# Idle TensorE products in the opening's waits, and vector steps put in another order, in a fused one-layer kernel

## What is computed

```python
sh1, sc1, g1, sh2, sc2, g2 = adaln(cond, w_ada, b_ada)     # SiLU(cond) @ w_ada + b_ada
h = modulate(x, norm1_g, sh1, sc1)                         # rmsnorm(x) * (1 + scale) + shift
qkv, z, bl, al, na, gt = split_in(h, w_in)
o_dn, s = deltanet_branch(qkv, z, bl, al, ...)             # chunked gated DeltaNet, 8 heads
o_na = na_latent(...)                                      # neighbourhood attention, 8 heads
x = x + g1 * ((sig(gA) * (o_dn @ w_pa) + sig(gB) * (o_na @ w_pb)) @ w_out)
x = x + g2 * swiglu(modulate(x, norm2_g, sh2, sc2), w1, w3, w2)   # 2816 hidden features
```

## Time and profile before

| what | value |
|---|---|
| timed, median of 3 runs | 1314.75 us (1313.21 to 1315.12) |
| profiled execution, its own time | 1316.9 us |
| span of its profile | 1315.1 us |
| mean granted TensorE clock | 0.993 |
| PE busy | 98% |
| PEld busy | 93% |
| DVE busy | 74% |
| ACT busy | 53% |
| POOL busy | 13% |

### The profile page before, as it was taken

One profiled execution on the slowest core, in us unless ns is written; L12 is line 12 of the kernel. 1 busy time (PEld: TensorE's weight loads), 2 busy tenths in 40 slices (PEclk: granted clock), 3 DMA queues, 4 the chain that ended last, 5 costly groups with the idle time before them and its releaser, 6 DMA issues.

```text
span 1315.1 us, 25980 instructions
## 1 busy us (share of the span) xinstructions
PE 1294.9 (98%) x9834; PEld 1220.3 (93%) x9834; DVE 971.0 (74%) x2230; ACT 700.5 (53%) x1578; POOL 171.1 (13%) x161
## 2 busy tenths in 40 slices
PE   6999999999999999999999999999999999999998
PEld 4898999999999999999988889999999999999998
DVE  6677867777685867767447666767999698987995
ACT  4564736465464646555366654437564355534643
POOL 1002020202002020200202220000103300041022
PEclk7999999999999999999999999999999999999999
DMA  9743534334143333315425225522323323233223
GB/s 313 238 129 96 163 103 118 109 101 117 48 136 101 114 103 96 98 53 149 145 72 191 67 77 167 159 61 57 87 75 97 91 70 97 65 97 97 76 61 105
DMA packets 207860, 144.59 MB, mean 110 GB/s; under 512 B 9471, under 2 KB 197159, under 8 KB 207607
## 3 DMA queue, kind: packets, MB, share of 16 engines
q1 hardware_dynamic: 207447, 142.79, 37.0%
q10 hardware_dynamic: 288, 0.13, 0.0%
HBM read 126.73 MB, written 17.99 MB: 110 GB/s over the span
## 4 chain that ended last, share of the span: by engine, by line
PE 93%; DVE 3%; DMA 1%; issue 1%; ACT 1%; SPq 1%; DVEq 0%; ACTq 0%
PE ps L1304 33%; PE ps L1927 26%; PE ps L1671 7%; PE ps L1586 3%; PE ps L1907 2%; PE ps L1278 2%; PE ps L1526 2%; PE ps L1593 2%; PE ps L1409 1%; PE ps L1605 1%; PE ps L1780 1%; PE ps L1766 1%; PE ps L1812 1%; PE ps L1886 1%; PE ps L1604 1%; PE ps L1664 1%
## 5 line engine op out<-in xcount | busy, mean ns | idle before, releaser
L1304 PE MATMUL ps<-hT_r,WAH_r 128*128 128x320 f32 x624 | 155.1, 330 | 0.0
L1304 PE MATMUL ps<-xT_r,WAH_r 128*128 128x320 f32 x624 | 142.5, 310 | 0.0
L1927 PE MATMUL ps<-d_part_r,W_r 128*128 128x320 f32 x660 | 136.8, 310 | 1.1 <-DVE xT L3365 0.7
L1304 PE MATMUL ps<-hT_r,W_r 128*128 128x320 f32 x592 | 134.7, 311 | 0.0
L1927 PEld LDWEIGHTS ps<-d_part_r,W_r 128*128 128x128 f32 x660 | 107.5, 188 | 2.2 <-DVE xT L3365 1.5
L1304 PEld LDWEIGHTS ps<-hT_r,WAH_r 128*128 128x128 f32 x624 | 100.9, 190 | 9.2 <-issue 8.2
L1927 PE MATMUL ps<-t_big_r,W_r 128*128 128x320 f32 x380 | 107.5, 310 | 0.9 <-DVE c L3341 0.7
L1304 PEld LDWEIGHTS ps<-xT_r,WAH_r 128*128 128x128 f32 x624 | 105.1, 189 | 0.0
L1927 PE MATMUL ps<-b_part,W_r 128*128 128x320 f32 x456 | 101.2, 309 | 0.0
L1304 PEld LDWEIGHTS ps<-hT_r,W_r 128*128 128x128 f32 x592 | 99.5, 190 | 0.1
L1927 PE MATMUL ps<-t_small_r,W_r 128*128 128x320 f32 x304 | 93.9, 309 | 0.0
(11 more groups left out here) (483 smaller groups left out, 3447.6 us busy)
## 6 DMA issues: line engine op xcount, KB each, us to landing
oT<-in_ffn_w SPq DMA_DIRECT2D x44, 512.0 KB, 5.1
W<-in_w_in SPq DMA_DIRECT2D x36, 512.0 KB, 4.7
WAH<-in_w_ada SPq DMA_DIRECT2D x16, 1024.0 KB, 7.3
naT<-in_w_in SPq DMA_DIRECT2D x24, 512.0 KB, 4.2
ext_dram<-naT SPq DMA_DIRECT2D x28, 320.0 KB, 4.1
oT<-in_ffn_w SPq DMA_DIRECT2D x32, 256.0 KB, 4.0
tA<-ext_dram SPq DMA_DIRECT2D x16, 320.0 KB, 4.1
GCB<-gc_dram SPq DMA_DIRECT2D x7, 640.0 KB, 4.6
```

Source lines behind the costliest of these rows:

```text
L1304: m = e.matmul(ps[:, bank + b, 0:n], w[:, k, :], x[:, k, a:a + n], start=k == 0 and i == 0, stop=k == KD - 1 and i == 2, skip_group_check= ...
L1927: m = e.matmul(ps[:, bank, 0:HT], w[i][:, k, :], x[i][:, k, :], start=start and k == 0 and j == 0, stop=k == half - 1 and j == 2, skip_gro ...
```

## The change

Seven places of the program are touched; GpSimd's and SyncE's instructions stay as they are.

1. **Opening, TensorE.** A new function `stay_busy(count)` issues `count` products of the 128 by 128 identity with itself into an unused PSUM bank, each in float32. There are 7 between the halves of `ada_group(0)`, 2 ahead of `ada_select(0)`, 9 behind it, and 4 between the first block of q and the second half of `ada_group(1)`. Nobody reads their results.
2. **Opening, ACT and DVE.** ACT puts the second modulation rows out of PSUM ahead of rounding the weights of k, and DVE norms tile 5 behind `small_h(3)` instead of ahead of `gains(1)`.
3. **Attention, ACT.** At three places `ln k` stands between the two copies `PT`, not behind both.
4. **Attention, DVE.** At step 13, `pa_lo_of` stands ahead of the steps `c rows`, `qz` and `kn`.
5. **Output projection.** PSUM banks come from a table `WO_BANKS`; TensorE's wait for the last sums of y is replaced by one on the bank's reader; `wo_lo_of(1)` moves from between `ysum` and `y_small` of tile 6 to behind all of `y_small`.
6. **Up turn 5.** The small parts of two hidden blocks move from ahead of the turn's sums to behind `C22`.
7. **First down turn of each round (g = 0).** The small part of S4 moves ahead of y12a and y22b, and y22a moves ahead of the small parts of A22 and D4.

```diff
+            def stay_busy(count):
+
+                for _ in range(count):
+                    e.matmul(ps[:, 4, 0:P], IDN, IDN, start=True, stop=True, skip_group_check=True)
...
-            ada_group(0)
+            first, second = range(0, KD // 2), range(KD // 2, KD)
+            ada_group(0, first)
+            stay_busy(7)
+            ada_group(0, second)
+            stay_busy(2)
             ada_select(0)
             e.wait_ge(vec_out, 1)
             e.wait_ge(rstd_done, 1)
-            first, second = range(0, KD // 2), range(KD // 2, KD)
+            stay_busy(9)
...
             blocks("q", 0)
+            stay_busy(4)
             ada_group(1, second)
...
-            e.wait_ge(y_sum, 2 * KD - 3)
             for n in range(KD):
                 e.wait_ge(wo_lo, n + 1)
-                if n >= 3:
+                if n == 2:
+                    e.wait_ge(wo_x, 1)
+                elif n >= 3:
...
+            ada_out_row(1)
             opening_big(OPENING_BIG["k"], W[:, slot["k"], :, :], ld_w["k"], 16)
-            ada_out_row(1)
...
                 if j:
                     copy_P(2 * j - 2)
+                for_next_pair(ACT_BETWEEN, j)
+                if j:
                     copy_P(2 * j - 1)
...
-                if n in (5, 6):
-                    wo_lo_of(n - 5)
+                if n == 5:
+                    wo_lo_of(0)
...
+            wo_lo_of(1)
             wo_lo_of(2)
...
                     hid_small(n - 1, "D3")
+                    sum_small(n, "S4")
                     result(n, "y12a")
                     result(n, "y22b")
-                    sum_small(n, "S4")
                     hid_small(n - 1, "B22")
+                    result(n, "y22a")
                     plain_small(n, "A22")
                     hid_small(n - 1, "D4")
-                    result(n, "y22a")
                     result(n, "y11b")
```

## The result

The changed kernel took 1317.44 us (median of 12 runs, 1316.66 to 1318.69), the kernel before 1315.16 us beside it (12 runs). The ratio is 1.0017, with a 95% interval of 1.0009 to 1.0025: slower by 2.2 us, between 1.2 and 3.3. That is inside the stated range and within 0.2%, though the interval's upper end is beyond 0.2%. The predicted 1315.3 was 2.1 us too low: 1.7 us of that is the change itself (+0.55 forecast, +2.2 measured), and 0.4 us the kernel before, which had 1314.75 in the forecast and 1315.16 here.

The account below looks back on a forecast made before the run. TensorE, busy 98% of the span, bounds the kernel, through its waits and clock. −1.0 − 1.2 − 0.65 − 0.2 + 0 + 3.6 + 0 = +0.55 us takes the median 1314.75 to 1315.3, range 1311.9 to 1318.3.

Parts of the forecast that it names:

- Rival C: First down turns, rounds 0 and 1: GpSimd's second sum goes ahead of S4, P7 starts 1.1 us late; 1317.5 us, chance 0.18.
- rival D: Opening: the clock falls all the same, in the unfilled wait for k's weights; about +3.0 us, 1318.3, chance 0.12.
- S4's own move: First down turn, round 0: S4 straight behind D3 holds nobody; P7's wait for y12a is just met (1002.45 against 1002.46).
- P4 late by about 0.8 us: First down turns, rounds 0 and 1: y22a waits for P7, A22 and D4 follow late, so P4 is late by 0.8 us.
- 1.0 us more of lag: First down turns: late DVE adds 0.4 and 0.6 us of waiting before the next turn's P6 and P7; 1.8 us a round.
- The last round 0: First down turn of the last round: no change in time, bounds −0.9 and +1.0 us.
- Opening -1.0: Opening: idle products keep the clock up, block k starts at 29.84 at the earliest, not 31.17; −1.0 us, bounds 0 and −1.33.
- Attention -1.2 and -0.65: Attention: ss 0.4 us sooner at three places, −1.2 us; DVE's subtraction moved into idle time ahead of nmx, −0.65 us.
- Output projection -0.2: Output projection: TensorE's start loses its wait, but DVE becomes the bound at tile 1's small weights; −0.2 us, bounds 0 and −0.5.
- Up turn 5: 0: Up turn 5: the pause for C22 nearly vanishes but comes back at the next sum; 0, bounds 0 and −0.8 us.
- rival A: Whole kernel: the forecast itself, within 0.2%, 1315.3 us, own range 1313.3 to 1317.4 by the rounds' price; chance 0.48.

Follow-up runs that it names:

- experiment 2: Two kernels, each the kernel before with one move of part 7: S4's small part directly behind D3's, 1.0021; y22a ahead of A22's and D4's small parts, 1.0019.
- experiment 4: The changed kernel, with GpSimd's second sum in the first down turns waiting for S4's small part: 0.9996 of the kernel before.
- experiment 6: The kernel before with S4's small part ahead of D3's, directly behind S3's: 1.0011 of the kernel before, +1.4 us.
- experiment 5: The kernel of experiment 4, with GpSimd's third sum also waiting for D4's small part in the first down turns: 1.0015 of the kernel before.
- experiment 3: The kernel before with S4's small part moved between y12a and y22b in the down turns: 1.0004 of the kernel before.

## Why the prediction was right, and where its steps failed

The class (within 0.2%) and the range were right; the centre was too low. That the class came right is partly luck. Rival C, given 0.18, is what happened, on top of the forecast's own lateness of P4, and it cost 2.3 us that the forecast's sum didn't have; the range was wide enough because C and D had been put into its upper end.

The table sets the sum beside the profiles: by how much the same product of TensorE starts later (+) or sooner (-) from one end of a stage to the other than in the profile of before. "Others" are the further profiles that have the same part of the change.

| stage | forecast, us | changed kernel | others |
|---|---|---|---|
| opening (parts 1, 2) | -1.0 | -2.7 | -2.0 to -2.6 |
| attention (parts 3, 4) | -1.85 | -2.0 | -2.1 to -2.5 |
| output projection (part 5) | -0.2 | -0.5 | -0.1 to -0.6 |
| up turns (part 6) | 0 | -0.1 | -0.1 |
| first down turn, round 0 (part 7) | +1.8 | +2.25 | +2.26 (part 7 alone) |
| first down turn, round 1 | +1.8 | +2.45 | +2.44 |
| first down turn, last round | 0 | +0.4 | +0.4 |

1. *"S4's own move: nobody is held by it in round 0 if it goes straight behind D3."* This step failed. S4 took 1.78 us, P7 was 1.13 us late in two rounds: rival C's 1.1. Experiments 2, 4 and 6 show the cause: S4 is held while GpSimd's second sum runs. At this place the sum was issued 0.13 us ahead of S4, and S4 was held in all six cases (rounds 0 and 1 of the changed kernel, of part 7 alone and of S4's move alone). I let the one counterexample of the earlier trace rows weigh too much. The profile of before holds the opposite case too. In round 1 the sum was issued 0.33 us into the subtraction ahead of it (1159.31), and the next subtraction took its usual 0.68 us. In round 0, with the same instructions in the same order, the sum was issued 0.34 us into the subtraction ahead (1011.27), and the next one was held:

```profile
1011.61 1.50 POOL L3597 TENSOR_TENSOR oT<-oT 128x512 f32<-128x512 f32 x1 [3.52 <-PE ps L1927]
...
1011.87 1.78 DVE L3223 TENSOR_TENSOR oT_r<-oT,W_r 128x512 fp32r<-128x512 f32 x1
```

2. *P4 late by about 0.8 us.* Right: 0.83 us in both rounds, through y22a's wait for P7 and the hold by the third sum (experiments 2 and 5).
3. *1.0 us more of lag before the next turn's P6 and P7.* Mis-sized: 0.2 us (0.3 with the product behind the pause). So the forecast's 1.8 for a round would have been 1.0 to 1.2 without the hold of S4, and the two errors, of opposite sign, partly cancel: by timing part 7 cost 5.3 us (3.7 to 7.0) where the forecast had 3.6.
4. *The last round 0.* It measured +0.4 us, inside the bounds.
5. *Opening -1.0.* The mechanism was right in the profile (block k at 29.76, granted clock 1.00, rival D refuted). The size depends on what it is compared with: -2.7 us against the profile of before, about -0.7 against the mean of the seven profiles with the old opening, and by timing -0.1 us (-1.3 to +0.9), so timing doesn't exclude the -1.0. The step that failed is "from 22.85 to 31.17, TensorE's work ran at about half the clock", taken as what every execution does. In five of the other six profiles with the old opening block k started at 29.27 to 29.93; only in the one at 0.52 did it start at 30.53. The sum also left out the second low stretch near 72 us, which cost the profile of before 1.3 us more.
6. *Attention -1.2 and -0.65.* By the profile 1.66 us from the three pauses and 0.67 from the one ahead of the scores, less 0.3 that came back at other waits. *Output projection -0.2*: the pause of 0.5 us was gone in the changed kernel, but it is gone in four of eight profiles without part 5 as well, so what part 5 gave isn't shown. The sum had left the last y_small at its old time while moving TensorE's start 0.5 us ahead, 5.6 us behind it; it came 5.05 us behind. *Up turn 5: 0*, right: 0.07 us.
7. Together parts 3 to 6 gave -1.6 us by timing (-0.4 to -2.8), against -2.05 in the sum: no contradiction.

The measured parts add up: -2.5 (parts 1 to 6) and +5.3 (part 7) make +2.8, against +2.2 measured, with intervals of 1.1 us on either side for the first and third and 1.7 for the second.

A slip in the prediction's bounds changes nothing above: rival A's "own range" by its own terms (-3.05, with 1.5 to 6.0 for the rounds) is 1313.2 to 1317.7, not 1313.3 to 1317.4.

The Trainium skill (SBUF — State Buffer, "Who interferes with whom") says that issue order decides which of the two engines is blocked; that the first one keeps the access for its whole instruction it says of VectorE's two-port modes. By that rule C would have been certain. At the holds of S4, D3 and A22 the traces agree (1.78, 1.57 and 1.29 us). They don't everywhere: the earlier trace rows and the pair above went different ways, and in the last round a sum issued at 1269.11 took 2.66 us while the three subtractions issued behind it ran at their usual length (0.55, 0.49 and 0.55 us).

## What to carry to other kernels

Before moving a two-input SBUF instruction to a new place on VectorE, look at what GpSimd issues at that moment; an instruction that reads PSUM was not held there (experiment 3), though the subtraction that moved then met another sum, and nothing was gained in the end. A move that shortens the pause of one place (the last round, by 0.3 us) can be paid for in the other places that share the code (rounds 0 and 1, by 0.4 and 0.6 us), so it should be made only where it helps. A pause that is gone in one profile proves little if it comes and goes without the change. And what one profile shows of a granted clock or of a landing DMA is one draw: compare several before it is put into a sum.

## What the runs showed of the hardware

- A subtraction on VectorE with both inputs in SBUF took 0.68 us alone and 1.78 us where GpSimd's sum was issued 0.13 us earlier; a result's step that reads PSUM (0.66 us) wasn't lengthened by the same sum. GpSimd's sum can also be the one that waits, 2.66 us for 1.0. Where the sum is issued 0.33 us into one subtraction and another follows at once, both came about with the same instructions in the same order (1.78 us at 1011.87, 0.68 at 1159.91). What decides between the two wasn't settled.
- The same opening ran at granted clocks from 0.51 to 0.88 between 17 and 31 us in different executions, with waits on DMAs of up to 2.4 us in it. With 22 idle products in four of these waits it was 1.00 in all seven profiles, and stayed so across an unfilled wait of 1.4 to 1.7 us ahead of block k in six of them.
